# Convolution layers: the next pair's accumulators begun within the pair, 11 GpSimd taps, two z units behind the pairs, sums later; three small orders elsewhere

## The reference

```python
def conformer_conv_mixer(h, w_in, conv_w, conv_b, ln_g, ln_b, w_out):
    proj = h @ w_in                                   # 1024 -> 3 * 2048
    val, glu_gate, z = jnp.split(proj, 3, axis=-1)
    u = val * jax.nn.sigmoid(glu_gate)
    u = causal_depthwise_conv(u, conv_w) + conv_b     # 31 taps, per channel
    u = jax.nn.silu(layer_norm(u, ln_g, ln_b))        # over the 2048 channels
    return (u * jax.nn.silu(z)) @ w_out               # 2048 -> 1024
```

## Time and profile before

| | us |
|---|---|
| median of 3 runs (lowest, highest) | 1822.97 (1818.86, 1827.63) |
| the profiled execution | 1822.21 |
| its span | 1820.4 |
| PE busy in it | 1747.3 (96%) |
| DVE busy | 1444.4 (79%) |
| ACT busy | 1075.1 (59%) |
| POOL busy | 328.9 (18%), nearly all in the two convolution layers |
| granted PE clock, mean | 0.99 |

### The profile page before, as it was taken

How to read it: one execution, slowest core, us unless ns; L and a number is a source line. 1 busy time by engine, 2 the same in 40 slices (tenths; PEclk the granted TensorE clock), 3 DMA queues, 4 the chain that set the end, 5 groups by cost and what they waited for, 6 DMA issues and landing times.

```text
span 1820.4 us, 30985 instructions
## 1 busy us (share of the span) xinstructions
PE 1747.3 (96%) x11636; PEld 1579.0 (87%) x11636; DVE 1444.4 (79%) x2710; ACT 1075.1 (59%) x2047; POOL 328.9 (18%) x412
## 2 busy tenths in 40 slices
PE   7998999999999999999989999999999999999997
PEld 6887788888889999988877989889998998889996
DVE  7999777877778878789978688787777778787667
ACT  6898665555454444468975556565555556565554
POOL 2999000000000000079940000020000200030000
PEclk9999999999999999999989999999999999999999
DMA  6444458855558888644445554546765444546551
GB/s 227 142 149 151 142 180 306 277 194 167 195 196 290 295 289 291 208 154 151 130 128 196 164 193 132 162 153 192 243 212 172 144 146 126 169 135 220 189 181 72
DMA packets 92741, 339.62 MB, mean 187 GB/s; under 512 B 10288, under 2 KB 10672, under 8 KB 91952
## 3 DMA queue, kind: packets, MB, share of 16 engines
q1 hardware_dynamic: 92592, 337.64, 56.3%
HBM read 336.55 MB, written 1.05 MB: 185 GB/s over the span
## 4 chain that ended last, share of the span: by engine, by line
PE 60%; DVE 17%; ACT 11%; issue 9%; POOL 2%; DMA 0%; SPq 0%; DVEq 0%; ACTq 0%; POOLq 0%
PE ps L103 58%; DVE wl L119 6%; ACT tmp L109 5%; ACT wh L112 3%; POOL B L119 2%; DVE B L119 2%; DVE ps L129 2%; PE ps L106 1%; DVE tmp L119 1%; DVE tmp L129 1%; DVE raw L129 1%; ACT B L109 1%; ACT os L112 1%; ACT XS L112 1%; ACT ps L109 1%
## 5 line engine op out<-in xcount | busy, mean ns | idle before, releaser
L103 PE MATMUL ps<-XS,wh 128*128 128x256 f32 x4464 | 828.7, 287 | 9.5 <-DVE wl L119 8.5
L103 PEld LDWEIGHTS ps<-XS,wh 128*128 128x128 f32 x4464 | 706.1, 193 | 25.2 <-issue 13.2
L119 DVE TENSOR_TENSOR wl<-raw,wh 128x1024 fp32r<-128x1024 f32 x481 | 591.8, 1257 | 119.5 <-ACT wh L112 118.3
L103 PE MATMUL ps<-XS,wl 128*128 128x256 f32 x2232 | 635.5, 285 | 0.0
L112 ACT CAST wh<-raw 128x1024 fp32r<-128x1024 f32 x481 | 486.7, 1045 | 149.5 <-PE ps L103 136.6
L103 PEld LDWEIGHTS ps<-XS,wl 128*128 128x128 f32 x2232 | 431.3, 193 | 0.1
L119 POOL TENSOR_TENSOR B<-B,tmp 128x237 f32<-128x237 f32 (+11 forms) x384 | 287.2, 787 | 645.0 <-ACT tmp L109 644.8
L103 PE MATMUL ps<-wh,os 128*128 128x512 f32 x864 | 284.1, 394 | 10.9 <-DVE os L119 6.8
L129 DVE SCALAR_TENSOR_TENSOR ps<-B,C,ps 128x254 f32<-128x254 f32 (+16 forms) x544 | 212.0, 470 | 7.5 <-ACT ps L109 7.4
L103 PEld LDWEIGHTS ps<-wh,os 128*128 128x128 f32 x864 | 162.4, 188 | 50.3 <-DVE os L119 11.5
L103 PE MATMUL ps<-B,raw 128*128 128x256 f32 x832 | 184.3, 381 | 1.1 <-ACT B L109 1.1
(11 more groups left out here) (157 smaller groups left out, 1620.5 us busy)
## 6 DMA issues: line engine op xcount, KB each, us to landing
raw<-in_w SPq DMA_DIRECT2D x628, 512.0 KB, 4.5
B<-in_ln SPq DMA_DIRECT2D x4, 1024.0 KB, 6.3
C<-in_cst SPq DMA_DIRECT2D x1, 1103.5 KB, 10.3
X<-in_x SPq DMA_DIRECT2D x2, 512.0 KB, 5.8
out_x<-X SPq DMA_DIRECT2D x4, 256.0 KB, 2.5
cb<-in_cb SPq DMA_DIRECT2D x1, 512.0 KB, 12.8
pos<-in_pos SPq DMA_DIRECT2D x1, 160.0 KB, 2.3
raw<-in_w SPq DMA_DIRECT2D x1, 128.0 KB, 3.0
```

The costliest lines, as they stand in the source:

```text
L103: return NOTHING if self.e is None else self.e.matmul(*a, **k)
L119: return NOTHING if self.e is None else self.e.tensor_tensor(o, a, b, op)
```

## The change

In both convolution layers:
- POOL_TAPS goes from 12 to 11, so tap 11 moves from ScalarE and GpSimd to VectorE, and the order of `taps()` follows.
- ScalarE's item 0 becomes `begin(p)`: pair 0's stands before the loop, and pair p+1's behind item 25 of pair p, before the last two GpSimd products of that pair.
- The z units inside the pairs are four (pairs 2, 3, 5, 6) instead of six (pairs 1 to 6); z2 follows behind pair 7's v, in front of z3. The Silus and the feeds of z4 to z6 are placed anew, z6.1's feed last.
- TensorE's stats(7) moves in front of z6's first unit; on ScalarE stats(7) moves in front of the Silu of z4.

Elsewhere: `feed_dve` doesn't look further than the second piece of a coming layer (c, m0, f0, m1, f1); in the attention layer `turned(8)` is done two pieces earlier; in the mixers the quotients of softmax 15 are computed one step earlier, and branch bf6 is done in two halves, one in step 16, one in step 17.

```diff
-POOL_TAPS = 12
+POOL_TAPS = 11
+EARLY_Z = (2, 3, 5, 6)
...
+        self.firsts = [self.at[n] for n in ("c.c0.0", "m0.wr", "f0.u0.0.0", "m1.wr", "f1.u0.0.0")]
...
     def feed_dve(self, dve, name, look=LOOK):
-        while self.lows <= min(self.at[name] + look, len(self.pieces) - 1):
+        at = self.at[name]
+        last = min([at + look, len(self.pieces) - 1] + [first + 1 for first in self.firsts if first > at])
+        while self.lows <= last:
...
@@ pe_a
-            if 1 <= p < 7:
-                pair("z", (p - 1) // 2, ((p - 1) % 2,))
+            if p in EARLY_Z:
+                x = EARLY_Z.index(p)
+                pair("z", x // 2, (x % 2,))
+        pair("z", 2)
         pair("z", 3)
         stats(5)
         table(6)
         pair("z", 4)
         stats(6)
         pair("z", 5)
+        stats(7)
         pair("z", 6, (0,))
-        stats(7)
...
@@ act_a
+        def begin(p):
+            act.wait_ge(*s["conv"][A, "v", p])
+            if p >= 2:
+                act.wait_ge(*s["conv"][A, "done", p - 2])
...
+        begin(0)
         for p in range(8):
             items(p, 0, 4)
             if 1 <= p < 7:
                 self.feed_act(act, f"{A}.v{p + 1}.1", 0)
-            if p == 7:
-                self.feed_act(act, f"{A}.z5.0", 0)
             items(p, 4, 10)
             if p < 7:
                 gate(p + 1)
             else:
-                silu_z(3)
-                self.feed_act(act, f"{A}.z5.1", 0)
+                self.feed_act(act, f"{A}.z5.0", 0)
+                silu_z(2)
             items(p, 10, 14)
-            self.feed_act(act, f"{A}.v{p + 2}.0" if p < 6 else f"{A}.z{2 * p - 8}.0", 0)
-            if p in (2, 4, 6):
-                silu_z(p // 2 - 1)
+            self.feed_act(act, f"{A}.v{p + 2}.0" if p < 6 else f"{A}.z{p - 2}.{p - 6}", 0)
+            if p in (4, 6):
+                silu_z(p // 2 - 2)
...
             if p >= 6:
-                self.feed_act(act, f"{A}.z{2 * p - 8}.1", 0)
-            items(p, 22, 30)
+                self.feed_act(act, f"{A}.z{2 * p - 8}.{7 - p}", 0)
+            items(p, 22, 26)
+            if p < 7:
+                begin(p + 1)
+            else:
+                silu_z(3)
+            items(p, 26, 30)
+        self.feed_act(act, f"{A}.z6.1", 0)
+        stats(7)
         silu_z(4)
         self.feed_act(act, f"{A}.z7.0", 0)
-        stats(7)
...
@@ dve_a (z5.0 from behind item 7 to 13, z5.1 from 13 to 19, z6.0 from 19 to 27, z6.1 behind conv_end(7))
@@ act_b, dve_b
-                if 3 <= j - 3 and kp == 2:
+                if 3 <= j - 3 and kp == (2 if j < 11 else 0):
                     turned(j - 3)
...
@@ pe_m
-            if n in (11, 13, 15, 17):
+            if n in (11, 13, 15):
...
+            if n >= 16:
+                pe.wait_ge(*s["evac"][M, "gate", 7])
+                self.branch(pe, f"{M}.bf6", self.gate_bank(3), self.YA, (M, 0), (n - 16,))
...
@@ dve_m
-            if 1 <= n < 17:
+            if 1 <= n < 16:
                 self.dve_quotients(dve, self.tmp[2 + (n - 1) % 4], self.stat(n - 1), (M, n - 1))
...
+            if n == 15:
+                self.dve_quotients(dve, self.tmp[2 + n % 4], self.stat(n), (M, n))
```

More of the change, by code:

```diff
@@ L212, in plan_a @@
         two("v", p, 0, "split" if p else "plain")
-        if 1 <= p < 7:
-            out += z_unit(p - 1)
-    for x in range(6, 16):
+        if p in EARLY_Z:
+            out += z_unit(EARLY_Z.index(p))
+    for x in range(len(EARLY_Z), 16):
         out += z_unit(x)
@@ L838, in act_a @@
         npool = 0
+        def begin(p):
+            act.wait_ge(*s["conv"][A, "v", p])
+            if p >= 2:
+                act.wait_ge(*s["conv"][A, "done", p - 2])
+            for i in (2 * p, 2 * p + 1):
+                u, o = U[:, i % 8, :], self.ps[p % 2][:, (i % 2) * T:(i % 2) * T + T]
+                act.activation(o[:, 0:1], self.c(b_conv, i), ACT.Identity)
+                act.activation(o[:, 1:T], u[:, 0:T - 1], ACT.Identity, scale=self.c(w_conv, 29 * 16 + i),
+                               bias=self.c(b_conv, i)).then_inc(s["tap"].up((A, i, 29)), 1)
+            for i in (2 * p, 2 * p + 1):
+                act.activation(V[:, i, :], U[:, i % 8, :], ACT.Identity,
+                               scale=self.c(w_conv, 30 * 16 + i)).then_inc(s["tap"].up((A, i, 30)), 1)
         def item(p, n):
@@ L842, in item @@
             if n == 0:
[L843 to L853, removed]
                 return
@@ L1014, in dve_a @@
                 self.feed_dve(dve, f"{A}.v{p + 1}.1", 0)
-            if p == 7:
-                self.feed_dve(dve, f"{A}.z5.0", 0)
             items(p, 8, 14)
@@ L1019, in dve_a @@
             if p == 7:
-                self.feed_dve(dve, f"{A}.z5.1", 0)
+                self.feed_dve(dve, f"{A}.z5.0", 0)
             items(p, 14, 20)
@@ L1024, in dve_a @@
                 val(p + 1)
-            self.feed_dve(dve, f"{A}.v{p + 2}.0" if p < 6 else f"{A}.z{2 * p - 8}.0", 0)
+            self.feed_dve(dve, f"{A}.v{p + 2}.0" if p < 6 else f"{A}.z{p - 2}.{p - 6}", 0)
             items(p, 20, 28)
@@ L1028, in dve_a @@
             if p >= 6:
-                self.feed_dve(dve, f"{A}.z{2 * p - 8}.1", 0)
+                self.feed_dve(dve, f"{A}.z{2 * p - 8}.{7 - p}", 0)
             items(p, 28, 30)
         conv_end(7)
+        self.feed_dve(dve, f"{A}.z6.1", 0)
         self.feed_dve(dve, f"{A}.z7.0", 0)
@@ L1446, in act_b @@
                     self.feed_act(act, f"{name}.{kp}")
+                if 3 <= j - 3 and kp == (2 if j < 11 else 0):
+                    turned(j - 3)
                 if 3 <= i and kp < 2:
@@ L1450, in act_b @@
                     self.act_root(act, self.b_norm(i)[2], self.b_norm(i)[1], ("b", i))
-                if 3 <= j - 3 and kp == 2:
-                    turned(j - 3)
             if j < 3:
@@ L1921, in gate_bank, with branch @@
         return (g + 1) % 4
-    def branch(self, pe, name, bank, Y, y0):
+    def branch(self, pe, name, bank, Y, y0, us=range(2)):
         i, wh, wl = self.weights(pe, name)
-        for u in range(2):
+        for u in us:
             o = self.ps[bank][:, u * T:u * T + T]
@@ L1932, in branch @@
                 ins = pe.matmul(o, wl[:, a:a + 128], Y[k][:, 0:T], start=False, stop=k == 3)
-        ins.then_inc(self.s["gemm"].up(i, name), 1)
+        if us[-1] == 1:
+            ins.then_inc(self.s["gemm"].up(i, name), 1)
     def pe_m(self, pe, l):
@@ L2215, in act_m @@
                         s["evac"].up((M, "gate", n // 2)), 1)
-            if n in (11, 13, 15, 17):
-                self.feed_act(act, f"{M}.bf{n - 11}")
+            if n in (11, 13, 15, 16):
+                self.feed_act(act, f"{M}.bf{n - 11 if n < 16 else 6}")
             if n == 1:
```

## The result

The changed kernel takes 1828.07 us (median of 20 runs, 1823.82 to 1836.62) against 1820.41 for the kernel before in the same session (1818.36 to 1827.63): ratio 1.0046, 95% interval 1.0037 to 1.0056, so 8.4 us slower. The forecast was 1821.5, a hair faster, with 1818 to 1825 as its own range and 1811.5 to 1829 as the range over all its cases. The profiled execution took 1832.51 with a span of 1830.7, 4.4 us above the median of its kernel, and lies in the upper of two groups: 13 runs at 1823.8 to 1829.1 and 7 at 1832.5 to 1836.6.

What follows compares the result with a forecast made beforehand. TensorE, busy 96% of the span, was taken as the bound. Convolution layers +2.5, attention -1.2, mixers -2.5, look-ahead +0.5 sum to -0.7 from 1822.2: 1821.5 us; own range 1818 to 1825, all cases 1811.5 to 1829.

Steps and rivals of the forecast that it cites:

- part 3: Convolution layers, z2 and z3 behind v7: z3 waits some 4 us for z2's Silu; both layers +2.5 us.
- without the wait for z3, -4.9: Low end for the two convolution layers: -4.9 us if z3 follows z2 without waiting for its Silu.
- The clock's price: Low TensorE clock behind the wait in front of z3: 1.7 us in each convolution layer.
- The listed signs: Expected in the changed profile: 4 us TensorE wait before z3, no 6.6 us wait for squares, GpSimd busy down 21 to 30.
- The tail: Convolution layers, from sums(7) to the first output product: 13.6 us, against 13.7 and 15.3 before.
- Part 1: Convolution pairs, one tap from GpSimd to VectorE: VectorE 6.2 us more per layer, GpSimd 10.7 to 17.4 less; VectorE sets the pace.
- GpSimd ends within a microsecond: End of pair 7: GpSimd finishes before VectorE's last tap at 179.2 or within a microsecond of it.
- Part 2: Next pair's accumulators begun within the pair: VectorE's waits for them, 2.6 and 2.0 us in the two layers, go.
- Part 4: Small orders outside the convolution pairs: attention -1.2, mixers -2.5, weight look-ahead at layer starts +0.5 us.
- The clock inside the pairs: Shorter waits at v4.1 and v5.1 (2.5 to 3.4 us) would cost clock, but TensorE has slack: nothing in the sum.
- The bank-7 loop closes: Rival: z2 starts late, z5.0 lands late, delaying the Silu and z3, with longer low clock: +8, 1827 us; chance 0.18.

Runs made afterwards that it cites:

- small_only: The kernel before with the small orders alone (look-ahead limit, turned(8) earlier, softmax 15 quotients earlier with bf6 halved): 1818.14 us, ratio 0.9982.
- before_taps11: The kernel before with 11 GpSimd taps instead of 12, nothing else: 1820.17 us, ratio 0.9991.
- nobegin_taps12: The changed kernel with begin(p+1) put back behind the last product of pair p and 12 GpSimd taps: 1835.74 us, ratio 1.0078.
- after_cast_late: The changed kernel with z4.0's cast in pair 6 moved from item 14 to 22, its subtraction from 20 to 28: 1821.72 us, ratio 1.0007.
- silu_early: The changed kernel with z1's Silu in front of z4.0's cast and z2's in front of pair 7's accumulators: 1819.35 us, ratio 0.9994.
- taps12_after: The changed kernel with GpSimd's 12 taps again: 1859.13 us, ratio 1.0220.
- silu_z1_only: The changed kernel with z1's Silu alone moved in front of the cast of z4.0: 1824.61 us, ratio 1.0029.

## Why the prediction was wrong

**The failed step: part 3, "From there ScalarE has ..."** The sum took +2.5 us for the two layers, the runs give 11.7. I walked ScalarE from val(7) on, as if it were ready for pair 7's accumulators when val(7) is there, and so started behind pair 6, where the new wait stands: the cast of z4.0 for v7.1. The walk itself was right, 7.05 us from the accumulators at 157.38 to z2's Silu at 164.43 against 7.1; its start was not, since val(7) had been done at 153.02, 4.4 us before. With the cast moved the accumulators start at 150.98, 0.5 us behind val(7). I checked that z5.0's buffer of `raw` comes free in time, and never asked the same of `wh`. Two z units moved behind v7.1 put it two places earlier, from piece 37 of the layer to 35 (counted from 0), and leave z4.0 at 40: both are 0 modulo 5 now. Before, the piece five places ahead of z4.0 was g7.1, a plain one that takes no `wh`.

What it did, by the forecast's own clock times in the first layer:

| | forecast | measured |
|---|---|---|
| val(7) | 154.6 | 152.34 |
| v7.1 done | 150.8 | 149.96 |
| z2 starts | 150.8 | 153.06, clock 0.79 over 8 us |
| z2's Silu | 161.7 | 164.43 |
| z3 starts | 162.4 | 165.07 |
| sums(7) | 184.4 | 185.19 |
| first output product | 198.0 | 200.21 |

z3's wait for z2's Silu was foreseen and priced (4.3 and 4.4 us; 3.19 and 5.06 came), but z2's own wait of 3.10 us in both layers was not. The forecast's end "without the wait for z3, -4.9" is 7.4 below its +2.5; with the Silus early 9.5 were gained, with the cast late 7.1, both Silus together with begin back 15.8 (1.0046 to 0.9959). The clock's price was right in size, 1.7 us for each layer: z2 took 8.83 instead of 7.17 in the first, z3 8.70 in the second. That one of the two stood at z2 was not foreseen.

The listed signs did not catch the error: a wait of some 4 us in front of z3 and none of 6.6 for the squares were seen as forecast, and none of the signs asked for a wait in front of z2.

**A second term stood at nothing: operations kept out.** Part 1 priced the meeting of VectorE and GpSimd at stretched additions alone. In the profiled execution the first layer lost 3.7 us where +1.5 was forecast, the second 10.5 where it was +1.0, and some 6 of these are the comparison of 8.18 us. In the median this share is not known (see above).

**The tail was 1.4 short.** I took 13.6 us from sums(7) to the first output product; it is 15.0. Of this 0.8 is the spread's own time (192.06 to 192.86, where z7 starts), which I left out between z6.1 and "spread to first output product", since 6.7 to 6.8 are counted from its end; the rest is VectorE's first norm, 0.6 us behind the spread, because a subtraction whose cast stands behind a table load is in front of it.

**Part 1 held in what it moved.** GpSimd's busy time fell by 32.7 us. The forecast's 21 to 30 is short of its own price: 10.7 to 17.4 us a layer make 21 to 35. VectorE has its 32 instructions more. The tap alone costs nothing that can be told. But "GpSimd ends within a microsecond" was wrong: VectorE waited 3.08 us for it. ScalarE stood 4.70 us before the squares of pair 6, since TensorE's sums(5) now come behind z2 and z3, and GpSimd's last products stand behind those squares. That is part 3 again.

The warning that I set against part 1 was in the right place. The Trainium skill (Perfetto Trace Analysis, "Optimizing Scalar/DVE Operations") says that VectorE and GpSimd share an SBUF port; the Trainium skill's page SBUF — State Buffer, section "SBUF: two separate sides", says that whoever starts first holds it "for the whole instruction". By that rule a VectorE operation stays out for the rest of one addition, which takes 0.65 us. The three traces of the old order of ScalarE and the z units (before, small_only, before_taps11) agree: no such operation of the pairs was over 0.56 us late. In the traces of the other kernels it was up to 19 additions. The measurement decides.

**Part 2 was sized wrong.** The waits of VectorE for accumulators went, as forecast: in the first layer only that of pair 0 is left, 1.4 us. But I priced begin by the work behind it on ScalarE (hidden by 4 us) and not by ScalarE's wait itself: in the pairs of the first layer ScalarE waited 11.5 us for VectorE's products of v, 3.4 before (columns: total, times, longest):

```profile
ACT ps L110 <- DVE B L120: 11.5, 5, 5.0
ACT wh L113 <- PE ps L104: 8.5, 3, 4.5
```
```profile
ACT ps L109 <- DVE B L119: 3.4, 1, 3.4
```

begin is worth +3.3 us in the changed kernel and, with the spread told above, +17.7 in the old one, where I had -2.6 and -2.0 for the two layers. How much of that is ScalarE's wait and how much the operations kept out was not separated.

**Part 4 held in its sum, in part by luck.** Forecast -3.2, measured -3.3. The terms, by matmuls of the same number in the traces of before and after: attention -1.5 (-1.2) and c's start -0.4 (-0.3), each mixer -1.4 (-1.25), m1's start with its rope -0.3 where I had +0.9, f0 and f1 +0.6 each where I had -0.2 for both: there an 0.82 us wait for `os` is new. The errors at m1 and at f0 and f1 cancel.

**The clock inside the pairs.** The forecast let shorter waits inside the pairs cost clock and nothing in the sum. They did cost clock: in the first layer 2.42 us in front of 74.58 were followed by 0.58 over 4 us, and 2.59 us at 111.17 by 0.62, while 3.19 us in front of z3 were followed by 1.00. So the length of a wait alone did not decide. What these stretches cost in the end was not tried.

**The rivals.** "The bank-7 loop closes" at 1827 comes nearest in time, and its mechanism is kin (z2 late, low clock under it, everything behind it later), but its trigger, z5.0's load, is not what happened: that its number is so near is luck.

## What to carry to other kernels

When pieces share ring buffers by number, moving one piece changes who waits for whom in every ring: write down for each later piece whose buffer it takes, in each ring, and walk the engine from there, not from the last landmark that looks settled. A Silu that releases TensorE should not stand behind an instruction that waits for TensorE: here a cast of 1.04 us held it for 4.46. Where GpSimd runs unbroken beside VectorE operations that read two SBUF operands, look at the spread of the runs before the median, and look for single VectorE instructions many times their own length.

## What the hardware showed

A VectorE tensor_tensor with both inputs in SBUF, 0.68 or 1.21 us undisturbed, can stay out until GpSimd's run of additions ends: 12.83, 11.24, 10.05, 9.47, 8.18 us in five cases, in each of which it ended after GpSimd had stopped. Two more, 7.75 and 8.52 us in nobegin_taps12, got in within a run without a visible pause, where GpSimd's next product was ready only 0.08 us before its addition began. In the kernel before GpSimd's run is as unbroken (37 additions in the row above), and every one of these operations got in at the next addition, 0 to 0.6 us later. What decides between the two is open. It is not how early GpSimd's next product is ready: VectorE was let in where that lay up to 3.3 us ahead, and kept out where it lay 0.3. In four kernels (changed, after_cast_late, silu_early, taps12_after) the first comparison of pair 1 of the second layer was hit (8.18, 8.18, 6.27 and 10.05 us), but not in silu_z1_only (0.68), which has the changed kernel's order in that layer up to there; the phase of the two engines may have a part in it, and was not tried. Operations of the pairs that read or write PSUM with one operand were never hit in these traces: in the changed kernel's none of the 576 taps took over 0.49 us, and no product or sum of 512 columns over 0.69.
